# Token gates as one 256-column product per token, high and low part side by side, beside unpaired expert-up units

## The chip, the cores and the metric

The kernel runs on one core of a Trainium2 chip. The metric is device time in microseconds (us); lower is better. TensorE (PE) multiplies matrices: stationary weights are loaded (PEld) and the columns of the other operand stream through them into a PSUM bank (8 banks of 512 fp32 columns). VectorE (DVE), ScalarE (ACT) and GpSimd (POOL) do the elementwise work, SyncE (SP) issues the DMA loads. Each engine works its own list of instructions in order, and engines wait for each other on semaphores.

## The reference

Two transformer blocks over 256 tokens of width 1024. The first ones (attention, MLP, convolution, retention, block attention) are not touched. The last layer is a mixture of 16,384 single-neuron experts, addressed by a pair of keys (i1, i2) of 128 each; each token picks 16 experts per head of 8 heads:

```
def peer(h, w_q, sub_keys, u_tab, v_tab):
    ...
    experts = jnp.take_along_axis(cand_i, pos, axis=-1)      # i1 * 128 + i2, 128 per token
    gates = jax.nn.softmax(top_s, axis=-1).astype(h.dtype)
    def one_chunk(args):
        hc, ec, gc = args
        a = jax.nn.gelu(jnp.einsum('td,thkd->thk', hc, u_tab[ec]), approximate=False)
        return jnp.einsum('thk,thkd->td', gc * a, v_tab[ec])
```

## The kernel before, in words

All weights come as 540 "units" of 128x1024 fp32 through a ring of four slots. The kernel keeps fp32 accuracy with one-pass fp32r products: ACT rounds a unit to its high part (`unit_hi`, L488), POOL or DVE makes the low part as the difference (`unit_lo`, L494), and PE adds three products high x high, high x low, low x high. `h_tile` (L549) does so with 24 products of 256 columns.

Instead of gathering experts, the kernel computes all of them densely. `act_e` holds 128 tiles of 128 experts x 256 tokens: tile n holds gelu(h.u) of the experts whose second key is n. It is then multiplied by a dense matrix of gates, zero for experts not picked, and multiplied with the v table (128 units `peer_v`, L614).

The gate matrix of one token, 128 x 128, is the product of two one-hot matrices over its 128 picks: `hot1` (pick x first key) and `hot2` (pick x second key, times the gate). DVE builds them four tokens at a time, a *group* (`one_hots`, three operations of 512 elements; 64 groups, two buffers in turn), PE multiplies (`token_gates`, L1255, four products of 128 columns in plain fp32), and DVE applies the group to `act_e` (`gate_tokens`): it multiplies the tiles already there (units 0 to n-1) and copies the gates of the tiles still to come. Tiles that come later are multiplied as they arrive (`gate_unit`).

The order is written out by hand. Of the 128 expert-up units (`peer_u`), 44 run before any group. Then follow 84 *gated units* k = 0..83, with four groups in every five units (`groups_before`): PE does group, unit, group, unit, group, unit, group, unit, unit. A gated unit goes through `h_pair_tile`: 8 products of 512 columns (L561: the high part of the weights by the high and low part of h side by side) and 8 of 256 (L567). It leaves two halves in its bank, 4 or 5, which DVE adds (`unit_sum`, L2717) into bank 6 or 7, where ACT takes the gelu (L1793 for the tokens already gated, L1795 into `act_e` for the rest). The groups use PSUM banks 0, 1 and 2 in turn, one bank for each. On DVE an iteration is: wait for the group's bank, make the one-hots of group g+2 into the buffers that group g has left, `gate_tokens(g)`, `gate_unit(k-1)`, `unit_sum(k)`.

Of the kernel before, what the change touches and what calls it, by code (L numbers as in the profile page):

```python
# [25 lines left out]
ALU = mybir.AluOpType  # L26
# [3 lines left out]
P = 128  # L30
T = 256
# [17 lines left out]
HOT_BANKS = 3  # L49
# [163 lines left out]
def build(nc, stream, x_t, x_rows, ctx_t, params, consts, decay, lam_in, rel_bias, onehot, dist_mask, scale_w, aside_w, c_rows, ln_rows,  # L213
          bias_rows, gate_cols, out):
    with ExitStack() as ctx:
# [32 lines left out]
        h_span = rounded("h_span", "arena", [P, (at["h"] - at["arena"]) // 4 + KC * T])  # L248

        def h_part(like, skip=0):  # L250

            first = (at[like] - at["arena"]) // 4 + skip
            return h_span[:, first:first + KC * T].rearrange("p (a b) -> p a b", a=KC)

        h_lo = h_part("h")
        gate_r = rounded("gate_r", "gate_lo", [P, T])
        e_pair = rounded("e_pair", "late", [P, 4, 2 * T], 2048)
# [32 lines left out]
        h_hi_1, h_hi_2, h_hi_3 = h_part("arena", 10752), h_part("arena", 19456), h_part("late")  # L290
        def h_parts(like, skip):

            first = (at[like] - at["arena"]) // 4 + skip
            apart = (at["h"] - at["arena"]) // 4 - first
            views = []
            for kc in range(KC):
                a = h_span[:, first + kc * T:first + (kc + 1) * T]
                views.append(bass.AP(a.tensor, a.offset, [a.ap[0], [apart, 2], [1, T]]))
            return views

        h_parts_1, h_parts_2, h_parts_3 = h_parts("arena", 10752), h_parts("arena", 19456), h_parts("late", 0)
# [60 lines left out]
        hot1, hot2 = ([a[:, at:at + 4 * P].rearrange("p (t e) -> p t e", t=4) for a, at in places] for places in (  # L362
            ((late, 2048), (cst, CONST["cos_2d"])), ((late, 3072), (cst, CONST["mean_64"]))))
# [23 lines left out]
        gate_ps = ps[:, 3, P:P + T]  # L387
# [7 lines left out]
        iota16_ps = ps[:, 7, 0:TOPK]  # L395

# [77 lines left out]
        unit_gelu = sem("unit_gelu")  # L474
# [25 lines left out]
        def _(pe):  # L500
# [39 lines left out]
            def h_tile(u, h_hi, bank, i=None):  # L540

                w_hi, w_lo = split_unit(u, i)
                start_fill(bank)
                for w, x in ((w_hi, h_hi), (w_hi, h_lo), (w_lo, h_hi)):
                    if w is w_lo:
                        wait_unit_lo(u, i)
                    for kc in range(KC):
                        begin = w is w_hi and x is h_hi and kc == 0
                        m = pe.matmul(ps[:, bank, 0:T], w[:, kc * P:(kc + 1) * P], x[:, kc, :], start=begin,  # L549
                                      stop=w is w_lo and kc == KC - 1)  # L550
                        if begin:
                            m.then_inc(units_begun, 1)
                m.then_inc(full[bank], 1)
                fills[bank].add()

            def h_pair_tile(u, parts, h_hi, bank, i=None):

                w_hi, w_lo = split_unit(u, i)
                start_fill(bank)
                for kc in range(KC):  # L560
                    m = pe.matmul(ps[:, bank, :], w_hi[:, kc * P:(kc + 1) * P], parts[kc], start=kc == 0, stop=False,  # L561
                                  skip_group_check=True)
                    if kc == 0:
                        m.then_inc(units_begun, 1)
                wait_unit_lo(u, i)
                for kc in range(KC):
                    m = pe.matmul(ps[:, bank, 0:T], w_lo[:, kc * P:(kc + 1) * P], h_hi[:, kc, :], start=False,  # L567
                                  stop=kc == KC - 1, skip_group_check=True)
                m.then_inc(full[bank], 1)
                fills[bank].add()  # L570
# [655 lines left out]
            def peer_u_pair(n):  # L1226
                h_pair_tile(FIRST_UNIT["peer_u"] + n, h_parts_3, h_hi_3, 4 + n % 2)

# [20 lines left out]
            def token_gates(g):  # L1249

                b = g % HOT_BANKS
                pe.wait_ge(hot_ready, g + 1)
                start_fill(b)
                for t in range(4):
                    m = pe.matmul(ps[:, b, t * P:(t + 1) * P], hot1[g % 2][:, t, :], hot2[g % 2][:, t, :], start=True, stop=True)  # L1255
                m.then_inc(full[b], 1)
                fills[b].add()

            for k in range(GATED_UNITS):
                for g in groups_before(k):  # L1260
                    token_gates(g)
                peer_u_pair(FIRST_GATED + k)
# [36 lines left out]
        def _(act):  # L1299
# [486 lines left out]
            for k in range(GATED_UNITS):  # L1786
                n = FIRST_GATED + k
                b = 4 + n % 2
                t = tokens_gated(k)
                unit_hi(act, FIRST_UNIT["peer_u"] + n + 2)  # L1790
                act.wait_ge(emptied[b], drains[b].add())
                total = ps[:, 6 + k % 2, 0:T]
                m = act.activation(total[:, 0:t], total[:, 0:t], ACT.Gelu)  # L1793
                if t < T:
                    m = act.activation(act_e[:, n, t:T], total[:, t:T], ACT.Gelu)  # L1795
                m.then_inc(unit_gelu, 1)
                if k >= GATED_UNITS - 3:
                    expert_hi(k - (GATED_UNITS - 3))
# [14 lines left out]
        def _(dve):  # L1813
# [845 lines left out]
            step(dve.tensor_copy(gate_hi[:, :], ps[:, 6, 0:T]))  # L2659
            settle()  # L2660
            dve.tensor_copy(gate_ps, gate_hi[:, :]).then_inc(emptied[6], 1)
# [4 lines left out]

            def one_hots(g):

                def of_tokens(a):
                    return a[:, 4 * g:4 * g + 4].unsqueeze(2).broadcast_to([P, 4, P])  # L2670

                iotas = spread(iota_ps, 4)
                step(dve.tensor_tensor(hot2[g % 2], iotas, of_tokens(i2_t), ALU.is_equal))
                dve.tensor_tensor(hot1[g % 2], iotas, of_tokens(i1_t), ALU.is_equal)
                settle()
                dve.tensor_tensor(hot2[g % 2], hot2[g % 2], of_tokens(gate_ps), ALU.mult).then_inc(hot_ready, 1)

            def gate_tokens(g, units):

                b = g % HOT_BANKS  # L2680
                gates = ps[:, b, :].rearrange("p (t e) -> p e t", t=4)
                a = act_e[:, :, 4 * g:4 * g + 4]
                dve.tensor_tensor(a[:, 0:units], a[:, 0:units], gates[:, 0:units], ALU.mult)
                dve.tensor_copy(a[:, units:N_EXP], gates[:, units:N_EXP]).then_inc(emptied[b], 1)
# [4 lines left out]
            def gate_unit(k):  # L2689

                n = FIRST_GATED + k
                t = tokens_gated(k)
                dve.wait_ge(unit_gelu, k + 1)
                last_group = t // 4 - 1
                dve.wait_ge(emptied[last_group % HOT_BANKS], reads[last_group % HOT_BANKS].n)
                dve.tensor_tensor(act_e[:, n, 0:t], ps[:, 6 + k % 2, 0:t], act_e[:, n, 0:t],
                                  ALU.mult).then_inc(unit_gated, 1)

            for g in range(2):
                one_hots(g)  # L2700
# [11 lines left out]
            def unit_sum(k):  # L2712

                n = FIRST_GATED + k
                b = 4 + n % 2
                dve.wait_ge(full[b], n_u[n % 2].add())
                dve.tensor_reduce(ps[:, 6 + k % 2, 0:T], ps[:, b, :].rearrange("p (a t) -> p t a", a=2), AX_X,  # L2717
                                  ALU.add).then_inc(emptied[b], 1)

            for k in range(GATED_UNITS):  # L2720
                for g in groups_before(k):
                    filled(g % HOT_BANKS)
                    if g + 2 < GROUPS:
                        one_hots(g + 2)
                    if k >= 1:
                        dve.wait_ge(unit_gelu, k)
                    gate_tokens(g, FIRST_GATED + k)
                if k >= 1:
                    gate_unit(k - 1)
# [3 lines left out]
            gate_unit(GATED_UNITS - 1)  # L2733
# [294 lines left out]
```

## Time and profile before

| | |
|---|---|
| median of 3 runs | 1877.89 us (1874.55 to 1877.93) |
| the profiled execution | 1875.69 us, of which its span is 1873.9 us |
| PE busy in the span | 1814.3 us, 97% |
| DVE, ACT, POOL busy | 1204.1, 859.8, 997.0 us |
| the stage of groups and gated units | about 1227.9 to 1520.6 us of the span |
| mean granted TensorE clock | 0.991 of full speed |

Busy time says which engine is full, not which wait decides. A row of the timeline is one instruction or a run of equal ones: its start, how long it took from the first start to the last end, and in brackets how long the engine had been idle and who ended that. PE and DVE begin an instruction before the one in front of it has ended, so what an instruction adds to the time of its engine is the distance between two starts, which is less than its duration.

### The profile page before, as it was taken

The numbers are of one execution on the slowest core, as the hardware profiler recorded it, in microseconds if no ns is written. First come the engines' busy times: TensorE is split into PE (matmuls) and PEld (weight loads), VectorE is DVE, ScalarE is ACT, GpSimd is POOL, SyncE is SP. The second block draws the span as 40 slices with busy tenths as digits, with TensorE's granted clock in tenths as the row PEclk, the third lists the DMA queues.
The fourth block names the chain that finished last, engine by engine and source line by source line (L and its number), as shares of the span: only waits on it lengthen the run. The fifth ranks groups of instructions, "written<-read, shape, count | busy, mean of one in ns | idle before, by whom it ended". The sixth has DMA issues, their size and how long they took to land.

```text
span 1873.9 us, 30601 instructions
## 1 busy us (share of the span) xinstructions
PE 1814.3 (97%) x10910; PEld 1554.6 (83%) x10910; DVE 1204.1 (64%) x2053; ACT 859.8 (46%) x1407; POOL 997.0 (53%) x431
## 2 busy tenths in 40 slices
PE   5999899998999999999999999999999999999999
PEld 2847579887979997988978899998999988888887
DVE  6587767788556545133233269978888867777776
ACT  3033554445445554542453546643344345554453
POOL 4043146443775444675438668876666654444443
PEclk8999999999999999999999999999999999999999
DMA  8787247786655554543324455544444455555554
GB/s 322 260 299 253 72 146 243 263 277 218 210 202 178 186 186 157 191 147 101 113 90 169 157 171 183 185 146 147 155 150 146 153 184 191 192 195 195 190 191 168
DMA packets 95319, 345.98 MB, mean 185 GB/s; under 512 B 10544, under 2 KB 12032, under 8 KB 94592
## 3 DMA queue, kind: packets, MB, share of 16 engines
q1 hardware_dynamic: 78048, 283.67, 45.2%
q10 hardware_dynamic: 17184, 61.11, 9.5%
q8 instruction: 59, 0.97, 0.2%
q14 instruction: 28, 0.23, 0.0%
HBM read 343.66 MB, written 1.08 MB: 184 GB/s over the span
## 4 chain that ended last, share of the span: by engine, by line
PE 82%; DVE 5%; issue 4%; DMA 4%; POOL 2%; ACT 2%; ACTq 0%; DVEq 0%; POOLq 0%; SPq 0%
PE ps L614 27%; PE ps L549 24%; PE ps L561 8%; PE ps L567 4%; PE ps L1255 3%; POOL ring_lo L494 2%; PE ps L770 2%; PE ps L837 2%; DMA ring<-stream 2%; PE ps L684 1%; PE ps L1000 1%; PE ps L533 1%; DMA arena<-aside_w 1%; DMA cst<-consts 1%; PE ps L784 1%
## 5 line engine op out<-in xcount | busy, mean ns | idle before, releaser
L494 POOL TENSOR_TENSOR ring_lo<-ring,ring_hi 128x1024 fp32r<-128x1024 f32 x371 | 896.8, 2422 | 691.7 <-ACT ring_hi L488 690.4
L488 ACT ACTIVATE ring_hi<-ring 128x1024 fp32r<-128x1024 f32 x502 | 531.2, 1059 | 442.5 <-DMA ring<-stream 438.5
L549 PE MATMUL ps<-h_span,ring_hi 128*128 128x256 f32 x2848 | 377.3, 286 | 0.2
L549 PEld LDWEIGHTS ps<-h_span,ring_hi 128*128 128x128 f32 x2848 | 360.5, 193 | 9.2 <-issue 4.7
L614 PE MATMUL ps<-ring_hi,e_pair 128*128 128x512 f32 x1024 | 253.8, 389 | 0.9 <-DVE e_pair L2707 0.9
L2707 DVE TENSOR_TENSOR e_pair<-arena,e_pair 128x256 fp32r<-128x256 f32 x128 | 174.9, 1367 | 99.3 <-ACT e_pair L1784 99.2
L614 PEld LDWEIGHTS ps<-ring_hi,e_pair 128*128 128x128 f32 x1024 | 192.1, 188 | 41.1 <-issue 1.3
L549 PE MATMUL ps<-h_span,ring_lo 128*128 128x256 f32 x1424 | 200.7, 284 | 0.7 <-POOL ring_lo L494 0.7
L494 DVE TENSOR_TENSOR ring_lo<-ring,ring_hi 128x1024 fp32r<-128x1024 f32 x141 | 175.5, 1245 | 37.5 <-ACT ring_hi L488 37.2
L549 PEld LDWEIGHTS ps<-h_span,ring_lo 128*128 128x128 f32 x1424 | 184.2, 193 | 1.5 <-POOL ring_lo L494 1.5
L614 PE MATMUL ps<-ring_hi,arena_r 128*128 128x512 f32 x672 | 174.5, 392 | 0.7 <-ACT ring_hi L488 0.7
L561 PE MATMUL ps<-h_span,ring_hi 128*128 128x512 f32 x672 | 174.6, 402 | 0.0
L2324 DVE CAST arena_r<-arena 128x256 fp32r<-128x256 f32 x64 | 78.1, 1220 | 111.8 <-ACT arena L1625 111.6
L614 PEld LDWEIGHTS ps<-ring_hi,arena_r 128*128 128x128 f32 x672 | 122.3, 189 | 24.5 <-ACT ring_hi L488 1.1
L561 PEld LDWEIGHTS ps<-h_span,ring_hi 128*128 128x128 f32 x672 | 120.3, 189 | 22.1
L614 PE MATMUL ps<-ring_lo,e_pair 128*128 128x512 f32 x512 | 137.5, 389 | 0.0
L614 PEld LDWEIGHTS ps<-ring_lo,e_pair 128*128 128x128 f32 x512 | 96.2, 188 | 19.9
L1793 ACT ACTIVATE ps<-ps 128x256 f32<-128x256 f32 (+39 forms) x84 | 22.6, 269 | 175.2 <-DVE ps L2717 175.2
L1337 ACT ACTIVATE arena<-ps 128x256 f32<-128x256 f32 (+2 forms) x118 | 45.4, 385 | 122.8 <-PE ps L549 111.0
L567 PEld LDWEIGHTS ps<-h_span,ring_lo 128*128 128x128 f32 x672 | 91.6, 189 | 7.2
L614 PE MATMUL ps<-ring_lo,arena_r 128*128 128x512 f32 x320 | 91.2, 393 | 4.8 <-POOL ring_lo L494 2.4
L567 PE MATMUL ps<-h_span,ring_lo 128*128 128x256 f32 x672 | 93.4, 282 | 0.0
(289 smaller groups left out, 2217.8 us busy)
## 6 DMA issues: line engine op xcount, KB each, us to landing
ring<-stream SPq DMA_DIRECT2D x540, 512.0 KB, 3.3
arena<-aside_w ACTq DMA_DIRECT2D x49, 512.0 KB, 4.7
late<-aside_w ACTq DMA_DIRECT2D x21, 512.0 KB, 5.1
resid<-aside_w ACTq DMA_DIRECT2D x10, 512.0 KB, 6.2
arena<-scale_w ACTq DMA_DIRECT2D x8, 512.0 KB, 16.0
arena<-ln_rows ACTq DMA_DIRECT2D x8, 512.0 KB, 5.0
arena<-gate_cols ACTq DMA_DIRECT2D x2, 1024.0 KB, 4.8
arena<-decay ACTq DMA_DIRECT2D x1, 1536.0 KB, 7.0
```

Source lines behind the costliest of these rows:

```text
L488: act.activation(ring_hi[:, s, :], ring[:, s, :], ACT.Copy).then_inc(hi_ready, 1)
L494: eng.tensor_tensor(ring_lo[:, s, :], ring[:, s, :], ring_hi[:, s, :], ALU.subtract).then_inc(lo_ready[s], 1)
L549: m = pe.matmul(ps[:, bank, 0:T], w[:, kc * P:(kc + 1) * P], x[:, kc, :], start=begin, stop=w is w_lo and kc == KC - 1)
L561: m = pe.matmul(ps[:, bank, :], w_hi[:, kc * P:(kc + 1) * P], parts[kc], start=kc == 0, stop=False, skip_group_check=True)
L567: m = pe.matmul(ps[:, bank, 0:T], w_lo[:, kc * P:(kc + 1) * P], h_hi[:, kc, :], start=False, stop=kc == KC - 1, skip_group_check=True)
L614: m = pe.matmul(ps[:, b, :], x[:, tt * P:(tt + 1) * P], w[:, half * 512:(half + 1) * 512], start=start, stop=stop, skip_group_check=True)
L770: m = pe.matmul(ps[:, bank, tt * P:(tt + 1) * P], hcat[:, kc, tt * P:(tt + 1) * P], w[:, kc * P:(kc + 1) * P], start=kc == 0, stop=kc == K ...
L837: m = pe.matmul(ps[:, b0 + tt, :], x[:, kc, tt * P:(tt + 1) * P], w[:, k2 * 512:(k2 + 1) * 512], start=begin and kc == 0, stop=w is w_lo a ...
L1255: m = pe.matmul(ps[:, b, t * P:(t + 1) * P], hot1[g % 2][:, t, :], hot2[g % 2][:, t, :], start=True, stop=True)
L1337: act.activation(dst, ps[:, b, 0:n], func, **kw).then_inc(emptied[b], 1)
L2324: dve.tensor_copy(hid_hi[:, j % 4, :], hid2[:, j % 4, :]).then_inc(hid_hi_ready, 1)
L2707: dve.tensor_tensor(e_lo[:, e % 4, :], act_e[:, e if row is None else row, :], e_hi[:, e % 4, :], ALU.subtract).then_inc(e_lo_ready, 1)
```

## The change

- `token_gates`: `hot2` now has 256 columns per token, the one-hot times the high part of the gate and the one-hot times its low part, all fp32r. The product of a token has 256 columns, so a group of four tokens fills two banks. The three banks are taken in pairs (0,1), (2,0), (1,2): each group shares its second bank with the group before it.
- `one_hots` has four operations of 512 elements where it had three; the gates lie in PSUM for half of the tokens at a time (`half_gates`, called twice).
- ACT copies the high halves out of PSUM: for tiles already there into a buffer `gate_part`, for the others into `act_e`.
- `gate_tokens` adds the low halves to the copies (two operations) and then multiplies. In groups whose banks are not neighbours (one in three) each operation is done in two pieces. The lower bank is freed by the multiplication, the higher one by a further step after it.
- The gated units go through `h_tile` (24 products of 256 columns) like all others. `unit_sum` is gone: ACT takes the gelu straight from bank 4 or 5. `gate_unit(k)` now stands in the same iteration as unit k.

```diff
-HOT_BANKS = 3
+HOT_BANKS = ((0, 1), (2, 0), (1, 2))
...
             def token_gates(g):
-                b = g % HOT_BANKS
                 pe.wait_ge(hot_ready, g + 1)
-                start_fill(b)
-                for t in range(4):
-                    m = pe.matmul(ps[:, b, t * P:(t + 1) * P], hot1[g % 2][:, t, :], hot2[g % 2][:, t, :], start=True, stop=True)
-                m.then_inc(full[b], 1)
-                fills[b].add()
+                for b in HOT_BANKS[g % 3]:
+                    start_fill(b)
+                    first = 2 * (b == max(HOT_BANKS[g % 3]))
+                    for t in range(2):
+                        m = pe.matmul(ps[:, b, t * T:(t + 1) * T], hot1[g % 2][:, first + t, :],
+                                      hot2_parts[g % 2][:, first + t, :], start=True, stop=True)
+                    m.then_inc(full[b], 1)
+                    fills[b].add()
...
-                peer_u_pair(FIRST_GATED + k)
+                peer_u_tile(FIRST_GATED + k)
...   (ACT)
+                for g in groups_before(k):
+                    for hb in HOT_BANKS[g % 3]:
+                        act.wait_ge(full[hb], mark["group", g][hb])
...
+                    for hi, _, tokens, part in group_parts(g):
+                        act.activation(part[:, 0:n], hi[:, 0:n], ACT.Copy)
+                        m = act.activation(tokens[:, n:N_EXP], hi[:, n:N_EXP], ACT.Copy)
+                    m.then_inc(group_copied, 1)
                 unit_hi(act, FIRST_UNIT["peer_u"] + n + 2)
-                act.wait_ge(emptied[b], drains[b].add())
-                total = ps[:, 6 + k % 2, 0:T]
-                m = act.activation(total[:, 0:t], total[:, 0:t], ACT.Gelu)
+                act.wait_ge(full[b], drains[b].add())
+                if k >= 2:
+                    act.wait_ge(unit_gated, k - 1)
+                m = act.activation(ps[:, 6 + k % 2, 0:t], ps[:, b, 0:t], ACT.Gelu)
...   (DVE)
-                dve.tensor_tensor(hot2[g % 2], hot2[g % 2], of_tokens(gate_ps), ALU.mult).then_inc(hot_ready, 1)
+                dve.tensor_tensor(lo, hi, of_tokens(gate_lo_ps, 4 * g % P), ALU.mult)
+                dve.tensor_tensor(hi, hi, of_tokens(gate_hi_ps, 4 * g % P), ALU.mult).then_inc(hot_ready, 1)
 
             def gate_tokens(g, units):
-                dve.tensor_tensor(a[:, 0:units], a[:, 0:units], gates[:, 0:units], ALU.mult)
-                dve.tensor_copy(a[:, units:N_EXP], gates[:, units:N_EXP]).then_inc(emptied[b], 1)
+                dve.wait_ge(group_copied, g + 1)
+                for hi, lo, a, part in group_parts(g):
+                    step(dve.tensor_tensor(hi[:, 0:units], lo[:, 0:units], part[:, 0:units], ALU.add))
+                for hi, lo, a, part in group_parts(g):
+                    dve.tensor_tensor(a[:, units:N_EXP], lo[:, units:N_EXP], a[:, units:N_EXP], ALU.add)
+                settle()
+                for hi, lo, a, part in group_parts(g):
+                    m = dve.tensor_tensor(a[:, 0:units], hi[:, 0:units], a[:, 0:units], ALU.mult)
+                m.then_inc(emptied[low], 1)
+                dve.wait_ge(emptied[low], mark["group", g][low])
+                dve.sem_inc(emptied[high], 1)
...
             for k in range(GATED_UNITS):
                 for g in groups_before(k):
-                    filled(g % HOT_BANKS)
+                    for b in HOT_BANKS[g % 3]:
+                        dve.wait_ge(full[b], mark["group", g][b])
                     if g + 2 < GROUPS:
                         one_hots(g + 2)
...
-                unit_sum(k)
+                gate_unit(k)
```

On PE, a group and the unit behind it, before (`late` holds the one-hots of a group; `emptied1` is bank 1 free again; `h_span` holds both parts of h):

```order
L1255 MATMUL ps<-late 128x128 [waits emptied2,hot_ready]
L1255 MATMUL ps<-late 128x128 x3
L561 MATMUL ps<-h_span,ring_hi 128x512 [waits emptied4,hi_ready]
L561 MATMUL ps<-h_span,ring_hi 128x512 x7
```

and of the changed kernel (`hot_parts` is the two-part `hot2`, `hot` is `hot1`, `late_r` and `h_lo` the two parts of h), a group, its unit and the group behind that:

```order
L1235 MATMUL ps<-hot_parts_a,hot_a 128x256 [waits emptied2,hot_ready]
L1235 MATMUL ps<-hot_parts_a,hot_a 128x256
L1235 MATMUL ps<-hot_parts_a,hot_a 128x256 [waits emptied0]
L1235 MATMUL ps<-hot_parts_a,hot_a 128x256
L547 MATMUL ps<-late_r,ring_hi 128x256 [waits emptied5,hi_ready]
L547 MATMUL ps<-late_r,ring_hi 128x256 x7
L547 MATMUL ps<-h_lo,ring_hi 128x256 x8
L547 MATMUL ps<-late_r,ring_lo 128x256 [waits lo_ready1]
L547 MATMUL ps<-late_r,ring_lo 128x256 x7
L1235 MATMUL ps<-hot_parts_b,hot_b 128x256 [waits emptied1,hot_ready]
L1235 MATMUL ps<-hot_parts_b,hot_b 128x256
L1235 MATMUL ps<-hot_parts_b,hot_b 128x256 [waits emptied2]
```

The four products of a group had one wait on a bank; now the third has a wait of its own, on the bank that the group before it used.

On DVE, one iteration before (tile 54, a group in it):

```order
L2673 TENSOR_TENSOR late<-ps,late 128x512 [waits full2]
L2674 TENSOR_TENSOR late<-ps,late 128x512
L2676 TENSOR_TENSOR late<-late,ps 128x512 [waits dve_step]
L2683 TENSOR_TENSOR arena<-arena,ps 128x54x4 [waits unit_gelu]
L2684 COPY arena<-ps 128x74x4
L2696 TENSOR_TENSOR arena<-ps,arena 128x32 [waits emptied1,unit_gelu]
L2717 TENSOR_REDUCE ps<-ps 128x256 [waits full4]
```

and of the changed kernel (a group with neighbouring banks):

```order
L2674 TENSOR_TENSOR hot_parts_b<-ps,late 128x4x128 [waits full1,full0]
L2675 TENSOR_TENSOR hot_b<-ps,late 128x512
L2677 TENSOR_TENSOR hot_parts_b<-hot_parts_b,ps 128x4x128 [waits dve_step]
L2678 TENSOR_TENSOR hot_parts_b<-hot_parts_b,ps 128x4x128
L2685 TENSOR_TENSOR ps<-ps,gate_part 128x77x4 [waits group_copied]
L2687 TENSOR_TENSOR arena<-ps,arena 128x51x4
L2690 TENSOR_TENSOR arena<-ps,arena 128x77x4 [waits dve_step]
L2706 TENSOR_TENSOR arena<-ps,arena 128x112 [waits emptied0,emptied5]
```

The operation that frees a bank of the group was the fifth (the copy) and is the seventh now; all that stand in front of it wait until the whole group is out of PE.

## Rows read from the trace of the kernel before

**Rows 1.** The page: span, busy time of the engines.
```profile
span 1873.9 us, 30601 instructions
PE 1814.3 (97%) x10910; PEld 1554.6 (83%) x10910; DVE 1204.1 (64%) x2053; ACT 859.8 (46%) x1407; POOL 997.0 (53%) x431
```

**Rows 2.** Busy time by stretch (us): engines, granted clock, DMA.
```profile
1240.00:1280.00 40.00, 40.00 (x252) 35.81 (x251) 32.07 (x68) 16.42 (x36) 26.34 (x12) 1.00 0.45 148
1440.00:1480.00 40.00, 40.00 (x255) 35.93 (x255) 34.72 (x69) 16.44 (x36) 27.31 (x12) 1.00 0.45 145
920.00:960.00 40.00, 37.29 (x243) 29.79 (x241) 12.34 (x38) 19.89 (x50) 15.25 (x7) 1.00 0.27 93
```

**Rows 3.** PE's timeline in the stage: start, length, instruction.
```profile
1227.92 1.06 PE L1255 MATMUL ps<-late 128*128 128x128 f32 x8
...
1301.99 1.05 PE L1255 MATMUL ps<-cst 128*128 128x128 f32 x8
1302.79 2.11 PE L561 MATMUL ps<-h_span,ring_hi 128*128 128x512 f32 x8
1304.74 1.11 PE L567 MATMUL ps<-h_span,ring_lo 128*128 128x256 f32 x8
1305.69 1.06 PE L1255 MATMUL ps<-late 128*128 128x128 f32 x8
...
1506.62 2.00 PE L561 MATMUL ps<-h_span,ring_hi 128*128 128x512 f32 x8
1508.46 1.12 PE L567 MATMUL ps<-h_span,ring_lo 128*128 128x256 f32 x8
1509.41 2.00 PE L561 MATMUL ps<-h_span,ring_hi 128*128 128x512 f32 x8
...
1520.59 2.00 PE L614 MATMUL ps<-ring_hi,e_pair 128*128 128x512 f32 x8
```

**Rows 4.** PE's timeline among the ungated, unpaired units.
```profile
1150.41 1.12 PE L549 MATMUL ps<-h_span,ring_lo 128*128 128x256 f32 x8
1151.37 2.08 PE L549 MATMUL ps<-h_span,ring_hi 128*128 128x256 f32 x16
1153.29 0.40 PE L549 MATMUL ps<-h_span,ring_lo 128*128 128x256 f32 x2
```

**Rows 5.** DVE's timeline, one iteration of the middle of the stage.
```profile
1303.08 0.69 DVE L2673 TENSOR_TENSOR cst<-ps,late 128x512 f32<-128x512 f32 x1 [0.19 <-PE ps L1255]
1303.68 0.68 DVE L2674 TENSOR_TENSOR cst<-ps,late 128x512 f32<-128x512 f32 x1
1304.28 0.68 DVE L2676 TENSOR_TENSOR cst<-cst,ps 128x512 f32<-128x512 f32 x1
1304.88 0.42 DVE L2683 TENSOR_TENSOR arena<-arena,ps 128x260 f32<-128x260 f32 x1
1305.21 0.41 DVE L2684 COPY arena<-ps 128x252 f32<-128x252 f32 x1
1305.54 0.22 DVE L2696 TENSOR_TENSOR arena<-ps,arena 128x68 f32<-128x68 f32 x1
1305.89 0.70 DVE L2717 TENSOR_REDUCE ps<-ps 128x256 f32<-128x512 f32 x1
```

**Rows 6.** DVE's timeline late in the stage.
```profile
1494.71 0.64 DVE L2683 TENSOR_TENSOR arena<-arena,ps 128x476 f32<-128x476 f32 x1
1495.27 0.19 DVE L2684 COPY arena<-ps 128x36 f32<-128x36 f32 x1
1495.38 0.40 DVE L2696 TENSOR_TENSOR arena<-ps,arena 128x240 f32<-128x240 f32 x1
```

**Rows 7.** ACT's timeline in the middle of the stage.
```profile
1302.92 0.21 ACT L1793 ACTIVATE ps<-ps 128x68 f32<-128x68 f32 x1 [2.30 <-DVE ps L2717]
1303.04 0.32 ACT L1795 ACTIVATE arena<-ps 128x188 f32<-128x188 f32 x1
1303.25 1.06 ACT L488 ACTIVATE ring_hi<-ring 128x1024 fp32r<-128x1024 f32 x1
```

**Rows 8.** The timeline around PE's restart after a wait on DVE.
```profile
1218.51 2.30 DVE L2652 TENSOR_TENSOR cst<-cst,small 128x128 f32<-128x128 f32 x1
1220.87 0.66 PE L1242 MATMUL ps<-cst 128*128 128x128 f32 x4 [0.22 <-DVE cst L2652]
```

**Rows 9.** DVE's timeline ahead of the first group.
```profile
1226.48 0.68 DVE L2676 TENSOR_TENSOR cst<-cst,ps 128x512 f32<-128x512 f32 x1
1229.11 0.69 DVE L2673 TENSOR_TENSOR late<-ps,late 128x512 f32<-128x512 f32 x1 [1.95 <-PE ps L1255]
```

More of the change, by code:

```diff
@@ L247, in build @@
         late_r = rounded("late_r", "late", [P, 2048])
[L248 to L255, printed above, removed]
+        h_lo = rounded("h_lo", "h", [P, KC, T])
         gate_r = rounded("gate_r", "gate_lo", [P, T])
+        hot2_parts = [rounded("hot2_parts_a", "late", [P, 4, 2 * P], 2048), rounded("hot2_parts_b", "cst", [P, 4, 2 * P], CONST["cos_2d"])]
+        hot1 = [rounded("hot1_a", "late", [P, 4, P], 3072), rounded("hot1_b", "cst", [P, 4, P], CONST["mean_64"])]
+        gate_part = sb("gate_part", [P, N_EXP, 4])
         e_pair = rounded("e_pair", "late", [P, 4, 2 * T], 2048)
@@ L288, in build @@
         rstd = area(30720, 2, 512)
[L290 to L301, printed above, removed]
+        h_hi_1 = arena_r[:, 10752:12800].rearrange("p (a b) -> p a b", a=KC)
+        h_hi_2 = arena_r[:, 19456:21504].rearrange("p (a b) -> p a b", a=KC)
+        h_hi_3 = late_r[:, :].rearrange("p (a b) -> p a b", a=KC)
         hid_hi = arena_r[:, 12800:13824].rearrange("p (a b) -> p a b", a=4)
@@ L386, in build @@
         iota_ps = ps[:, 3, 0:P]
-        gate_ps = ps[:, 3, P:P + T]
+        gate_hi_ps, gate_lo_ps = ps[:, 3, P:2 * P], ps[:, 3, 2 * P:3 * P]
         bn = ps[:, 4, 384:408].rearrange("p (t a b) -> p t a b", t=2, a=2)
@@ L395, in build, with group_parts @@
         iota16_ps = ps[:, 7, 0:TOPK]
+        def group_parts(g):
+            low, high = min(HOT_BANKS[g % 3]), max(HOT_BANKS[g % 3])
+            banks = [(low, 2)] if high == low + 1 else [(low, 1), (high, 1)]
+            views, first = [], 0
+            for bank, n in banks:
+                parts = ps[:, bank:bank + n, :].rearrange("p b (t a e) -> p e (b t) a", t=2, a=2)
+                tokens = slice(4 * g + first, 4 * g + first + 2 * n)
+                views.append((parts[:, :, :, 0], parts[:, :, :, 1], act_e[:, :, tokens], gate_part[:, :, first:first + 2 * n]))
+                first += 2 * n
+            return views
         landed = [sem(f"landed{s}") for s in range(RING)]
@@ L473, in build @@
         unit_gated = sem("unit_gated")
-        unit_gelu = sem("unit_gelu")
+        group_copied = sem("group_copied")
         dve_rows = sem("dve_rows")
@@ L552, in h_tile @@
                             m.then_inc(units_begun, 1)
[L553 to L568, printed above, removed]
                 m.then_inc(full[bank], 1)
@@ L1249, in token_gates @@
             def token_gates(g):
-                b = g % HOT_BANKS
                 pe.wait_ge(hot_ready, g + 1)
-                start_fill(b)
-                for t in range(4):
-                    m = pe.matmul(ps[:, b, t * P:(t + 1) * P], hot1[g % 2][:, t, :], hot2[g % 2][:, t, :], start=True, stop=True)
-                m.then_inc(full[b], 1)
-                fills[b].add()
+                for b in HOT_BANKS[g % 3]:
[6 more added lines that the diff above has]
+                    fills[b].add()
+                mark["group", g] = [fills[b].n for b in range(3)]
             for k in range(GATED_UNITS):
@@ L2665, in _, with half_gates, of_tokens @@
             dve.wait_ge(emptied[6], reads[6].n)
+            def half_gates(tt):
+                c = slice(tt * P, (tt + 1) * P)
+                dve.tensor_copy(gate_hi_ps, gate_hi[:, c])
+                step(dve.tensor_copy(gate_lo_ps, gate_lo[:, c]))
             def one_hots(g):
-                def of_tokens(a):
-                    return a[:, 4 * g:4 * g + 4].unsqueeze(2).broadcast_to([P, 4, P])
+                def of_tokens(a, first=4 * g):
+                    return a[:, first:first + 4].unsqueeze(2).broadcast_to([P, 4, P])
@@ L2678, in gate_tokens @@
+                dve.tensor_tensor(hi, hi, of_tokens(gate_hi_ps, 4 * g % P), ALU.mult).then_inc(hot_ready, 1)
             def gate_tokens(g, units):
[L2680 to L2684 removed]
+                low, high = min(HOT_BANKS[g % 3]), max(HOT_BANKS[g % 3])
@@ L2692, in gate_unit @@
                 t = tokens_gated(k)
-                dve.wait_ge(unit_gelu, k + 1)
+                dve.wait_ge(emptied[4 + n % 2], n_u[n % 2].add())
                 last_group = t // 4 - 1
-                dve.wait_ge(emptied[last_group % HOT_BANKS], reads[last_group % HOT_BANKS].n)
+                b = min(HOT_BANKS[last_group % 3])
+                dve.wait_ge(emptied[b], mark["group", last_group][b])
                 dve.tensor_tensor(act_e[:, n, 0:t], ps[:, 6 + k % 2, 0:t], act_e[:, n, 0:t],
                                   ALU.mult).then_inc(unit_gated, 1)
+            half_gates(0)
+            settle()
             for g in range(2):
@@ L2710, in expert_lo @@
                     unit_lo(dve, FIRST_UNIT["peer_v"] + e, i)
[L2712 to L2718, printed above, removed]
             for k in range(GATED_UNITS):
                 for g in groups_before(k):
-                    filled(g % HOT_BANKS)
+                    for b in HOT_BANKS[g % 3]:
+                        dve.wait_ge(full[b], mark["group", g][b])
+                    if g + 2 == GROUPS // 2:
+                        half_gates(1)
+                        settle()
                     if g + 2 < GROUPS:
                         one_hots(g + 2)
-                    if k >= 1:
-                        dve.wait_ge(unit_gelu, k)
                     gate_tokens(g, FIRST_GATED + k)
-                if k >= 1:
-                    gate_unit(k - 1)
-                unit_sum(k)
+                gate_unit(k)
                 if k >= GATED_UNITS - 3:
                     expert_lo(k - (GATED_UNITS - 3))
-            gate_unit(GATED_UNITS - 1)
             for e in range(3, 8):
```

21 lines of the change are left out of this document (11 added, 10 removed).

## The prediction

> **What bounds the kernel now.** I read the page first: PE is busy for 97% of the span, DVE for 64% [rows 1]. Then the stretches of the stage that is changed: in 40 us PE is busy for 40.00, at the full granted clock; DVE has 32 to 35 of 40, ACT 16, POOL 26 to 27 [rows 2]. So nothing but PE's own work sets the time of this stage, and DVE is the engine with the least room. PE's timeline gives the prices. From a group to the next it takes 1305.69 - 1301.99 = 3.70 us, one unit in between; without a group a unit takes 1509.41 - 1506.62 = 2.79 [rows 3]. So a group costs 0.91 us of PE. As a check, 84 units at 2.79 and 64 groups at 0.91 are 292.6; the stage lasts from 1227.92 to 1520.59, 292.7 [rows 3]. An unpaired unit of 24 products of 256 columns takes 1153.29 - 1150.41 = 2.88, 0.12 per product [rows 4].
>
> **PE's own work.** The trace has no fp32r product of one-hots; the nearest row is the 256-column product at 0.12 [rows 4]. A group of four is then 0.48 in place of 0.91: 64 x 0.43 = 27.5 us less. The bounds: it can't be much under 0.12 (the 512-column products have 0.23), and at worst it stays at 0.91, which I price below. Unpairing costs 84 x (2.88 - 2.79) = 7.6 us. The net for PE alone is -19.9 us. If nothing made PE wait, the time would be 1875.7 - 19.9 = 1855.8.
>
> **The work of DVE per group.** What an operation costs is the distance between starts: 0.60 for 512 elements, 0.33 for 260 or 252, 0.56 and 0.11 for 476 and 36 [rows 5, 6]. That is about 0.065 us and 1.04 ns per element; the end comes 0.09 after the next could start. All new forms (an add of PSUM and an SBUF buffer into PSUM or `act_e`) have one operand in PSUM and one in SBUF, as L2676 and L2683 have, and I take them at this rate. Gone is `unit_sum`, 0.6 per unit. New per group: a fourth one-hot operation (+0.60), and two adds and a multiplication where a multiplication and a copy were. With n tiles there (44 to 127, mean 84): adds of 4n and 512 - 4n elements, 0.41 + 0.25, then the multiplication of 4n, 0.41 to its next start and 0.50 to its end.
>
> **The new wait.** This decides, and it is not a matter of DVE's sum but of one loop. The second half of a group needs the bank that it shares with the group before, and DVE frees that bank only when it has applied the whole group. DVE starts on a group when both banks are full, a moment that I call F; and it makes the one-hots of group g+2 first. So the bank is freed at F + 4 x 0.60 (one-hots) + 0.41 + 0.25 (adds) + 0.50 (multiplication) = F + 3.56 at mean n; at n = 44 it is F + 3.34, at n = 124 F + 3.78. When does PE want it? F is 0.04 after the end of the last group product (DVE starts at 1303.08 on a group whose record runs from 1301.99 for 1.05 [rows 3, 5]). That product began 0.32 before F (a 256-column product takes 0.28 from start to end: 1.12 for eight at 0.12 [rows 4]), so the unit starts at F - 0.20, ends its pitch at F + 2.68, and two products later, at F + 2.92, PE comes to the third product of the next group. After a stalled group it is F + 2.86, since a product after a wait runs some 0.06 longer: the transposes at 1220.87 took 0.66 for four [rows 8]. PE restarts 0.05 after DVE's end (1218.51 + 2.30 = 1220.81 to 1220.87 [rows 8]). The wait is 3.56 + 0.05 - 2.86 = 0.75. One group in three works in halves (three more operations, 3 x 0.06) and hands on its higher bank, which is freed one step later (about 0.10, an estimate, bounds 0 and 0.2): +0.28 for a third of the groups, +0.09 in the mean. So 0.84 us for each wait.
>
> How often? Of the 64 groups, 48 come one unit behind the last group. For the other 16 there are two units in between, PE arrives 2.88 later, and there is no wait. 48 x 0.84 = 40.3 us. Behind the waiting product on PE stands the unit, and behind it everything; before, PE had no idle time here, so the wait goes into the end in full.
>
> **Small terms.** Behind a unit without a group DVE has to wait for ACT's gelu before `gate_unit`, which now stands in front of the next group: gelu is some 0.48 after the unit's end, as in rows 7 (0.44 from L1793's start to L1795's end), and `gate_unit` takes 0.06 to 0.33 (rows 6: 0.40 long for 240 elements). DVE is then late at a group by 0.02 to 0.26: 16 x 0.14 = 2.2. `half_gates(1)` adds 0.4 once. Ahead of the first group DVE gets four operations of one-hots twice instead of three and three more small ones, about 2.6 us in all; it was through at 1226.48 + 0.68 and waited for the group till 1229.11 [rows 9], so it comes some 0.7 us, at most 1.2 us, late to group 0: +1.2. Sum 3.8.
>
> **What hides.** ACT's copies of a group take 0.07 + 0.75 ns per element, by the start distances of L1793 and L1795 (0.12 for 68, 0.21 for 188 [rows 7]): 0.5 to 0.7 us, from F on. DVE asks for them at F + 2.40, so 1.7 us are to spare, and ACT's whole iteration (copies 0.6, `unit_hi` 1.06, gelu 0.44) is 2.1 of some 4. `unit_hi` comes 0.6 later, for a unit that is two units ahead; POOL's low part behind it too. Nothing changes in SP's queue but that the loads follow the slower units. In the stage behind (L614) nothing moves.
>
> **Sum.** -19.9 + 40.3 + 3.8 = +24.2 us, on the profiled execution's 1875.7: 1899.9. That execution lies 2.2 us under the median of the runs, 1877.9, so I keep to it within that and predict 1900.
>
> The Trainium skill ("VectorE: DVE Perf Modes", The DRAIN you can't avoid) says that the next VectorE operation can't issue before the pipe of the last one is empty. Here rows 5 say otherwise: L2674 starts at 1303.68 while L2673 runs till 1303.77. By the rule each of the seven operations would cost its full duration, 0.09 more, so some 0.5 us more per wait and 24 us in all; by the rows it costs nothing. The trace decides for the known forms, but where an operation waits on the one before it a part of this could come back, which is the first rival.
>
> **Rivals.**
> - *The hand-overs on DVE cost more.* The add that is waited for by the multiplication, the wait for ACT and the wait on its own result each cost a full end-to-start, 0.09 more than I count: 3 x 0.09 x 48 = 13 us, 1913. For: DVE has three waits inside `gate_tokens` where it had one. Against: the wait inside the one-hots costs nothing in rows 5 (0.60 again). Chance 0.15.
> - *The bank is free in time (faster).* If DVE were done by F + 2.8, PE would never wait and the gain of the products would stay: 1856. It decides from 0.75 us less than my chain has, that is more than one whole 512-element operation. For: DVE's sum per five units, 4 x (2.40 + 0.66 + 0.41) + 5 x 0.2 = 14.9, is under PE's 5 x 2.88 + 4 x 0.48 = 16.3, so an account by busy time says that it fits. Against: DVE can't begin before both banks are full, and rows 5 leave no room in the prices. Chance 0.10.
> - *Half of it.* If DVE's fixed part is 0.4 us less per group than I think, the waits lose 19 us and the result is 1881, about no change: 0.06.
> - *The one-hot products stay as long as they were.* PE's own work then falls by nothing on this term (+27.5), but PE arrives at the third product 0.2 later and fills the second half 0.2 later: the loop gets 0.21 longer, the 16 free groups 0.43: 1875.7 + 7.6 + 48 x (0.84 - 0.43 + 0.21) + 3.8 = 1917. Against: fp32r products of 256 columns have 0.12 in all of rows 4. Chance 0.04.
>
> The forecast itself has 0.65. What a measurement of this kernel can tell from no change is about 0.2%, 3.8 us. Faster by more than that: 0.11; within: 0.05; slower: 0.84. The forecast's own range is 1890 to 1910 (start distance 0.04 instead of 0.065 per operation gives -10; each hand-over between engines at nothing -7; +0.1 on each wait gives +5, +0.2 +10). With the cases at its sides I give 1882 to 1915.
>
> **What would show it.** Right: idle time of PE in front of the third of four group products, put down to DVE's multiplication in `gate_tokens`, some 0.6 us early and 1.1 us late in the stage, 48 times, 0 for groups after two units; group products 0.12 apart; the stage about 317 us long where it had 292.7. The granted clock stays full: PE's idle pieces are under 1.5 us, and with 7% idle it was 1.00 before [rows 2]. Wrong: PE without gaps there and a stage of 273 us; gaps in front of units (L547, which would be ACT's or POOL's doing) rather than of group products; or a DVE that waits for `group_copied`.

## The result

The changed kernel takes 1902.4 us (median of 4 runs, 1898.6 to 1904.3) against 1876.2 before (1870.8 to 1877.9): a ratio of 1.0139, with a 95% interval of 1.0116 to 1.0162. It is 1.4% slower. The forecast was 1900, with 1882 to 1915 as its range.

The page of the changed kernel, against [rows 1]: PE is busy for 8 us less, and the span is 25 us longer. So what was added is not work of PE but idle time.

```profile
span 1899.3 us, 31987 instructions
...
PE 1806.5 (95%) x11326; PEld 1564.5 (82%) x11326; DVE 1229.5 (65%) x2165; ACT 907.0 (48%) x1577; POOL 996.9 (52%) x431
```

The same stretches as in [rows 2], busy time of PE, PEld, DVE, ACT and POOL, then granted clock, DMA share and GB/s:

```profile
1240.00:1280.00 40.00, 36.55 (x295) 35.34 (x294) 31.77 (x79) 21.42 (x55) 24.68 (x12) 1.00 0.40 139
...
1440.00:1480.00 40.00, 34.97 (x281) 33.75 (x280) 33.73 (x75) 19.81 (x52) 24.63 (x11) 1.00 0.42 141
```

PE was busy for 40.00 of 40 before; it is now for 36.6 early and 35.0 late in the stage, at the full clock. DVE has no more busy time than before in these stretches, since it waits too. Who PE waits for, from 1225 to 1560 us (sum, times, longest):

```profile
PE ps L1235 <- DVE arena L2690: 21.5, 31, 1.2
PE ps L1235 <- DVEq L2693: 14.6, 16, 1.2
```

These are all of PE's waits in the stage: 47, all in front of a group product (L1235), 31 for the multiplication in `gate_tokens` (L2690), which frees the lower bank of a pair, and 16 for the step behind it (L2693), which frees the higher one. PE's timeline over two groups with two units before the first of them, to be put beside [rows 3]:

```profile
1379.22 0.64 PE L1235 MATMUL ps<-hot_parts_a,hot_a 128*128 128x256 f32 x4
1379.70 1.12 PE L547 MATMUL ps<-late_r,ring_hi 128*128 128x256 f32 x8
1380.66 1.12 PE L547 MATMUL ps<-h_lo,ring_hi 128*128 128x256 f32 x8
1381.62 1.12 PE L547 MATMUL ps<-late_r,ring_lo 128*128 128x256 f32 x8
1382.58 0.39 PE L1235 MATMUL ps<-hot_parts_b,hot_b 128*128 128x256 f32 x2
1383.72 0.51 PE L1235 MATMUL ps<-hot_parts_b,hot_b 128*128 128x256 f32 x2 [0.74 <-DVE arena L2690]
```

DVE's rows of the same stretch, which answer to [rows 5]:

```profile
1380.11 0.68 DVE L2674 TENSOR_TENSOR hot_parts_a<-ps,late 128x512 fp32r<-128x512 f32 x1
1380.71 0.68 DVE L2675 TENSOR_TENSOR hot_a<-ps,late 128x512 fp32r<-128x512 f32 x1
1381.31 0.68 DVE L2677 TENSOR_TENSOR hot_parts_a<-hot_parts_a,ps 128x512 fp32r<-128x512 f32 x1
1381.90 0.68 DVE L2678 TENSOR_TENSOR hot_parts_a<-hot_parts_a,ps 128x512 fp32r<-128x512 f32 x1
1382.50 0.51 DVE L2685 TENSOR_TENSOR ps<-ps,gate_part 128x336 f32<-128x336 f32 x1
1382.92 0.33 DVE L2687 TENSOR_TENSOR arena<-ps,arena 128x176 f32<-128x176 f32 x1
1383.17 0.50 DVE L2690 TENSOR_TENSOR arena<-ps,arena 128x336 f32<-128x336 f32 x1
```

The first group comes through in one piece, four products in 1379.70 - 1379.22 = 0.48 us: the products are as cheap as hoped. DVE starts on it at 1380.11 (0.2 us late, behind a `gate_unit`) and needs 3.56 us to the end of the multiplication at 1383.67. PE has been through the unit and two products of the next group by 1382.82 and starts the third at 1383.72, 0.90 us later; the bracket says 0.74, since it counts from the end of the product in front, not from where the next could have started.

### The profile page after: what moved, and what is told of

Read it like the earlier page. It is cut to its first block, busy times and chain, and to the rows that moved or that the text cites. A ratio compares the mean times of both kernels' runs of the same rounds, so it can differ in the third digit from the quotient of the medians.

```text
span 1899.3 us, 31987 instructions
## 1 busy us (share of the span) xinstructions
PE 1806.5 (95%) x11326; PEld 1564.5 (82%) x11326; DVE 1229.5 (65%) x2165; ACT 907.0 (48%) x1577; POOL 996.9 (52%) x431
## 4 chain that ended last, share of the span: by engine, by line
PE 78%; DVE 13%; DMA 3%; issue 2%; ACT 2%; POOL 2%; DVEq 0%; ACTq 0%; SPq 0%; POOLq 0%
PE ps L547 31%; PE ps L596 28%; PE ps L752 2%; PE ps L531 2%; PE ps L666 2%; PE ps L819 2%; POOL ring_lo L492 2%; PE ps L1235 2%; PE ps L766 2%; DMA ring<-stream 1%; PE ps L982 1%; DVE hot_parts_a L2674 1%; DVE ps L2685 1%; DVE arena L2690 1%; DVE hot_parts_a L2678 1%
## 5 line engine op out<-in xcount | busy, mean ns | idle before, releaser
L547 PE MATMUL ps<-h_lo,ring_hi 128*128 128x256 f32 x2096 | 295.2, 284 | 0.0
L547 PEld LDWEIGHTS ps<-h_lo,ring_hi 128*128 128x128 f32 x2096 | 271.4, 193 | 0.0
L547 PE MATMUL ps<-late_r,ring_lo 128*128 128x256 f32 x1136 | 159.4, 283 | 0.0
L547 PE MATMUL ps<-late_r,ring_hi 128*128 128x256 f32 x1136 | 159.4, 283 | 0.0
L547 PEld LDWEIGHTS ps<-late_r,ring_lo 128*128 128x128 f32 x1136 | 146.5, 192 | 0.2 <-POOL ring_lo L492 0.2
L547 PEld LDWEIGHTS ps<-late_r,ring_hi 128*128 128x128 f32 x1136 | 146.1, 191 | 0.2 <-issue 0.2
L547 PE MATMUL ps<-arena_r,ring_hi 128*128 128x256 f32 x960 | 139.5, 289 | 0.0
L547 PE MATMUL ps<-arena_r,ring_lo 128*128 128x256 f32 x960 | 135.2, 284 | 0.5 <-POOL ring_lo L492 0.5
L547 PEld LDWEIGHTS ps<-arena_r,ring_hi 128*128 128x128 f32 x960 | 128.8, 193 | 7.8 <-issue 3.4
L547 PEld LDWEIGHTS ps<-arena_r,ring_lo 128*128 128x128 f32 x960 | 124.1, 192 | 1.0 <-POOL ring_lo L492 1.0
L596 PEld LDWEIGHTS ps<-ring_lo,e_pair 128*128 128x128 f32 x512 | 96.1, 188 | 19.9
```

The source lines that it names most:

```text
L596: m = pe.matmul(ps[:, b, :], x[:, tt * P:(tt + 1) * P], w[:, half * 512:(half + 1) * 512], start=start, stop=stop, skip_group_check=True)
```

## The experiments

Theory A: the wait on the shared bank, 47 times, at the end of a chain that begins when the group is out of PE. Theory B: VectorE simply has too much work for the time PE needs. Stage means the time, in the profiled execution, from the first group product to the first product of the expert-down stage; "lost" is the sum of what the distances between PE's starts in it have over 0.12 us (left out where other forms of product stand in the stage). The two times of the kernel before are its medians beside e1 to e4 and beside e5 to e8, and the ratios go by the one that was measured together with the run.

| kernel | time, us | against before, 95% interval | stage, us | lost, us |
|---|---|---|---|---|
| before | 1875.8, 1876.9 | 1 | 292.7 | |
| changed | 1902.4 | 1.0139 (1.0116 to 1.0162) | 320.3 | 48.3 |
| e1 four banks | 1863.9 | 0.9937 (0.9920 to 0.9953) | 280.6 | 8.7 |
| e2 bank freed earlier | 1874.5 | 0.9990 (0.9975 to 1.0006) | 290.4 | 18.5 |
| e3 before, unpaired | 1882.6 | 1.0039 (1.0024 to 1.0053) | 298.8 | |
| e4 one more operation | 1930.4 | 1.0309 (1.0276 to 1.0342) | 352.0 | 79.6 |
| e5 four banks, paired | 1923.0 | 1.0243 (1.0226 to 1.0260) | 340.6 | |
| e6 applied first | 1867.5 | 0.9956 (0.9941 to 0.9971) | 282.6 | 10.6 |
| e7 no wait on own result | 1858.4 | 0.9904 (0.9888 to 0.9921) | 271.8 | 0 |
| e8 fewer groups late | 1856.0 | 0.9891 (0.9875 to 0.9908) | 271.8 | 0 |

### e1: no bank shared

```diff
-HOT_BANKS = ((0, 1), (2, 0), (1, 2))
+HOT_BANKS = ((0, 1), (2, 3))        # and g % 2 for g % 3
...
-        iota_ps = ps[:, 3, 0:P]
+        iota_ps = ps[:, 7, 0:P]       # the gates beside it, too
...
-                if k >= 2:
-                    act.wait_ge(unit_gated, k - 1)
-                m = act.activation(ps[:, 6 + k % 2, 0:t], ps[:, b, 0:t], ACT.Gelu)
+                if k >= 1:
+                    act.wait_ge(unit_gated, k)
+                m = act.activation(ps[:, 6, 0:t], ps[:, b, 0:t], ACT.Gelu)
```

> The changed kernel with four banks for the groups, in pairs (0,1) and (2,3), so that no group shares a bank with the group before it; the one-hot index row and the gates move to bank 7, and the gelus of the gated units all go through bank 6. VectorE's work is the same but for the operations in two pieces, which are gone (no pair is of distant banks). Theory A (PE waits because the third group product needs a bank that VectorE frees only at the end of its chain): the 47 waits go, PE's own work of 84 x 2.88 + 64 x 0.48 = 272.6 us is left of the stage's 320, so about 1855 us. Theory B (VectorE has more work than fits beside PE, whichever bank is used): the time stays within 6 us of the changed kernel, 1896 or more. Theory C (half and half: the bank is free, but VectorE's sum late in the stage, some 16.9 us for 16.3 of PE per five units, holds PE there): 1860 to 1870, with all waits after the middle of the stage.

Measured: 1863.9 us, 38 us under the changed kernel. The 47 waits are gone; what is left of PE's waits from the first group on is one line (10 waits, in front of the first product of a group), and the stretches of 100 us say where:

```profile
PE ps L1235 <- DVE arena L2690: 5.4, 10, 0.7
```

```profile
1300.00:1400.00 100.00, 99.46 (x829) 99.09 (x828) 90.72 (x199) 55.13 (x139) 72.02 (x30) 1.00 0.49 162
1400.00:1500.00 100.00, 94.89 (x774) 92.98 (x774) 88.58 (x182) 52.39 (x130) 68.96 (x29) 1.00 0.45 149
```

So A is right for 40 of the 48 us lost, and C, the mixed case, for the rest: 7.7 of the 8.7 us lost lie behind 1400 us, where a group costs VectorE most. B alone is out: the work was the same but for the pieces, which were some 0.2 us in every third group.

### e2: the bank freed earlier, the work unchanged

```diff
                     if g + 2 < GROUPS:
-                        one_hots(g + 2)
+                        one_hots(g + 2, range(2))
                     gate_tokens(g, FIRST_GATED + k)
+                    if g + 2 < GROUPS:
+                        one_hots(g + 2, range(2, 4))
```

(`ops` says which of the four one-hot operations are issued. A wait of VectorE for its earlier one-hots, once, ahead of `half_gates(1)`, belongs to the edit, too.)

> The changed kernel with the four one-hot operations cut in two: two of them before the group is applied, two after it. The three banks and the work stay as they are; only the bank is freed 2 x 0.60 us earlier. Theory A: the mean wait of 0.93 us (44 us in 47 waits) all but goes; left are the groups whose banks are not neighbours, late in the stage, 5 to 15 us in all, so 1860 to 1873 us. Theory B: 1900, as VectorE's sum is unchanged.

Measured: 1874.5, 28 us under the changed kernel, by nothing but order, and not clear of the kernel before (the interval takes in 1). It is 1.5 us over the range of A: 32 waits of 0.47 on the average are left, the more the further into the stage. A group in two pieces late in the stage shows it, and the row on PE behind it:

```profile
1444.12 0.65 DVE L2694 TENSOR_TENSOR arena<-ps,arena 128x210 f32<-128x210 f32 x2
```

```profile
1444.88 0.50 PE L1235 MATMUL ps<-hot_parts_a,hot_a 128*128 128x256 f32 x2 [0.67 <-DVEq L2697]
```

The pieces end at 1444.77, the higher bank is passed on 0.1 later, and PE, whose second product started at 1443.93, could have gone on at 1444.05. What the expectation left out is that the two operations put behind the release stand ahead of the next group: VectorE starts on this group at 1442.13, 1.0 us after its last product's end (1441.11), where it needed 0.1 in the changed kernel. So late in the stage most of the 1.2 us comes back as a later start, and VectorE's sum begins to decide.

### e3: the unpairing alone

```diff
-                peer_u_pair(FIRST_GATED + k)
+                peer_u_tile(FIRST_GATED + k)
...   (ACT)
+                act.wait_ge(full[b], drains[b].add())
+                m = act.activation(ps[:, 6 + k % 2, 0:t], ps[:, b, 0:t], ACT.Gelu)
...   (DVE)
-                unit_sum(k)
```

> The kernel before with the expert-up units unpaired alone: 24 products of 256 columns per gated unit, ScalarE takes the gelu straight from the unit's bank, VectorE's sum of the halves is gone; the groups stay as they are (one bank, plain fp32). By theory A and B alike it costs PE 84 x 0.09 = 7.6 us: 1884 us (1881 to 1887), no PE wait in the stage. If the unpaired units cost nothing beside fp32 groups: 1876.

Measured: 1882.6, 6.7 us more than before; its stage is 6.1 us longer. PE stays full, and VectorE has 24 us of 40 where it had 32:

```profile
1240.00:1280.00 40.00, 40.00 (x341) 40.00 (x340) 24.16 (x56) 16.86 (x35) 26.53 (x12) 1.00 0.44 146
```

This is the price that buys room on VectorE: 6 to 7 us of PE for 84 x 0.60 = 50 us of VectorE.

### e4: one more operation in the chain

```diff
                 step(dve.tensor_tensor(hi, iotas, of_tokens(i2_t), ALU.is_equal))
+                step(dve.tensor_tensor(lo, iotas, of_tokens(i2_t), ALU.is_equal))
```

> The changed kernel with a fifth one-hot operation of 512 elements per group (a comparison that the next operation overwrites), 0.60 us more on VectorE before the bank is freed. Theory A: each of the 46 to 48 waits gets 0.60 us longer, and the groups behind two units do not: +28 us, 1930. Theory B (VectorE's sum decides): each of the 62 groups gets 0.60 longer: +37 us, 1939. If VectorE did not decide at all: 1902.

Measured: 1930.4 us, +28.0 against the changed kernel, as A said (B said +37). PE's waits in the stage:

```profile
PE ps L1235 <- DVE arena L2691: 39.2, 29, 3.0
PE ps L1235 <- DVEq L2694: 22.9, 15, 1.8
```

Compared group by group, a wait is 0.60 us longer than in the changed kernel (the median of 44), and the groups behind two units wait for nothing in either, where B would have them wait, too. That tells A from B better than the time does. In sum the waits in front of the third product went from 43.4 us (47) to 69.1 (44). The other three, of groups 2, 27 and 54, have no wait since PE came late to them, slowed by a stretch at half its clock (see the last section). These stretches cost 5.7 us, and so this execution's stage is 31.7 us longer and not 26; its time is only 27.8 longer, as the stage began 4.0 us earlier.

### e5: the unpairing undone, on four banks

```diff
-                peer_u_tile(FIRST_GATED + k)
+                h_pair_tile(FIRST_UNIT["peer_u"] + FIRST_GATED + k, h_parts_3, h_hi_3, 4 + (FIRST_GATED + k) % 2)
...   (DVE)
+                    if k >= 1:
+                        dve.wait_ge(unit_gelu, k)
                     gate_tokens(g, FIRST_GATED + k)
-                gate_unit(k)
+                if k >= 1:
+                    gate_unit(k - 1)
+                unit_sum(k)
```

> The four-bank kernel (e1) with the unpairing undone: gated units again as 8 products of 512 and 8 of 256 columns, VectorE adds their halves (0.60 us per unit), ScalarE takes the gelu from the sum. PE's own work falls by 84 x 0.09 = 7 us. If PE alone decided: 1857. Theory A with C (VectorE's sum holds PE in the last third already): VectorE has 4 x 4.0 + 5 x 0.85 = 20.3 us per five units, against PE's 15.9, so PE waits throughout and the stage takes some 16 x 20.3 + 12 = 337 us: 1920 (1900 to 1940).

Measured: 1923.0, 59 us over e1, where PE had 7 us less to do. VectorE is the bound now. Its busy time does not tell: it is 90.5 of 100 us, as in e1 (90.7). But it no longer waits for PE; in these 100 us its waits are 4.3 us for its own results and 2.6 for ScalarE's gelu. PE waits for the sum of the halves (L2762), which frees a unit's bank:

```profile
1300.00:1400.00 100.00, 82.20 (x474) 70.76 (x473) 90.54 (x190) 44.03 (x112) 59.48 (x25) 1.00 0.41 132
```

```profile
PE ps L576 <- DVE ps L2762: 17.4, 15, 2.3
PE ps L1268 <- DVE arena L2721: 0.2, 1, 0.2
```

So wide gates and paired units don't go together in this order of VectorE's work, even with four banks; the unpairing is no side issue.

### e6: the group applied before any one-hot

The edit of e2 with `range(0)` ahead of `gate_tokens` and all four operations behind it.

> The changed kernel (three banks) with no one-hot operation before the group is applied and all four after it. The bank is freed 2.4 us earlier than in the changed kernel, but VectorE now waits for ScalarE's copies (some 0.75 us after the group) at each group. Theory A: no wait on the shared bank: 1862 to 1868, what is left being VectorE's sum. Theory B (VectorE's sum alone decides, and it is longer here by the waits for ScalarE): over 1900.

Measured: 1867.5. With three banks and the same operations, order alone takes 35 us off the changed kernel. The time is in A's range, but A had no wait on the shared bank, and 18 are left, 8.4 us, all from group 19 on: late in the stage VectorE now comes to most groups 2.0 to 2.3 us after their end, as it is still at the one-hots put behind the release (behind two units it is 0.9 to 1.0, the wait for ScalarE's copies). That each order of the same operations gives another time, 1902, 1874 or 1867, rules out B as the only cause.

### e7 and e8: the rest of VectorE's idle time

In e1 `gate_unit` stands 0.21 us behind the multiplication in front of it, since VectorE waits there for its own result:

```profile
1486.65 0.65 DVE L2690 TENSOR_TENSOR arena<-ps,arena 128x476 f32<-128x476 f32 x1
1487.52 0.41 DVE L2706 TENSOR_TENSOR arena<-ps,arena 128x244 f32<-128x244 f32 x1 [0.21 <-DVE arena L2690]
```

```diff
-                dve.wait_ge(emptied[low], mark["group", g][low])
-                dve.sem_inc(emptied[high], 1)      # PE takes the lower bank's release for both
+                if g >= GROUPS - 2:
+                    dve.wait_ge(emptied[low], mark["group", g][low])
+                    dve.sem_inc(emptied[high], GROUPS // 2)
...
-                dve.wait_ge(emptied[b], mark["group", last_group][b])
+                dve.wait_ge(rest_added, last_group + 1)
```

> The four-bank kernel (e1) without VectorE's wait for its own multiplication (0.21 us idle in front of gate_unit, 64 times): the lower bank's release stands for both banks, and gate_unit waits on the add instead. e1 loses 8.7 us of PE in 27 gaps, 7.7 of them in the last 100 us, where VectorE is the full engine. If so, 0.2 us per group there gives back most: 1857 to 1860. If the gaps are of another origin: 1864.

Measured: 1858.4, and not one wait of PE from the first group to the end of the stage, late in it neither:

```profile
1400.00:1500.00 100.00, 100.00 (x838) 100.00 (x837) 87.25 (x182) 58.54 (x135) 72.67 (x31) 1.00 0.50 165
```

Its 84 units and 64 groups take 271.8 us, which is PE's own work. e8 spreads the groups by another rule:

```diff
+def groups_up_to(k):
+    return min(GROUPS, -(-(900 * k - 13 * k * k // 10) // 1000))
...
-    return range(-(-4 * k // 5), min(GROUPS, -(-4 * (k + 1) // 5)))
+    return range(groups_up_to(k), groups_up_to(k + 1))
...
```

> e7 with the 64 groups spread another way over the first 81 gated units: nine in ten units at the beginning, seven in ten at the end, instead of four in five throughout, since a group costs VectorE 3.3 us at the beginning and 3.65 at the end. If VectorE's sum late in the stage is all that is left, no gap remains and PE's own work stands alone: 1855 to 1857. If the early groups, now with fewer units between them, overfill VectorE there: 1860 or more.

Measured: 1856.0, the same as e7 within their runs (e7 1855.98 to 1858.58, e8 1855.37 to 1864.99), with the same stage of 271.8 us. As e7 had no gap left, there was nothing for the other spreading to win, and this run says nothing on whether it would help where gaps are left. Both beat the kernel before by 1.0 to 1.1%.

## Why the prediction was right

The forecast was 1900 by one mechanism, and that mechanism is what the trace shows and the runs bear out. The time came closer than the terms did, by some luck: the stage is 320.3 - 292.7 = 27.7 us longer, where 24.2 were forecast (PE's own work fell by 1.0 more, the waits cost 4.2 more), but the profiled execution as a whole is only 1901.1 - 1875.7 = 25.4 longer. Term by term:

- *The group products, -27.5 us.* Right: from e3 to e7 the stage falls from 298.8 to 271.8, 27.0 us, and the two differ on PE in the group products alone.
- *The unpairing, +7.6 us.* Right, if a little too high: 6.1 us of stage, 6.7 of time in e3. PE's own work together was forecast at -19.9 and is 271.8 - 292.7 = -20.9.
- *VectorE's prices.* Right: F + 3.56 to the end of the multiplication at n = 84 is 1383.67 - 1380.11 = 3.56. For the two ends of the stage the forecast's own rate gives 3.40 and 3.73, not its 3.34 and 3.78; measured are 3.41 (group 3) and 3.72 (group 59). An operation that waits for another costs no more than the rest (the multiplication L2690, which waits for L2685, starts 0.25 behind L2687, the price of 176 elements). The first rival, dearer hand-overs on DVE, had its place in one spot only: 0.21 us idle in front of `gate_unit`, 62 times. It lies behind the release of the bank and cost PE nothing in nearly all groups, as DVE was back before the next group was out: it started 0.11 us after the end of 44 of the 46 stalled groups that have one-hots behind them. The other two are group 30 (`half_gates(1)`) and group 58 (0.33).
- *The waits, 48 x 0.84 us and 3.8 us besides, 44.1.* Mis-sized by a tenth: 48.3 us. There were 47 of them, as group 62 has no one-hots to make any more and the last group finds its bank free, at 0.92 us in front of the third product and 0.10 at the fourth, whose start is 0.22 behind the third's and not 0.12. I had taken 0.06 for a restart from four transposes [rows 8]; it is 0.10, and DVE comes to a stalled group 0.11 after PE's end, not 0.04.
- *How often.* Right: no wait for the groups behind two units (1379.22 above), growing from 0.6 us at the beginning of the stage (0.9 where the higher bank is waited for) to between 0.9 and 1.4 at its end, a third of them for the step on the higher bank (16 of 47). The first wait, 1.36 us, was the longest early one, as the late start of DVE had it.
- *The other rivals.* The bank is not free in time, and the busy-time account behind that rival (14.9 of 16.3 us per five units) shows its limit: that sum was about right (VectorE is busy for 90.7 of 100 us in the middle of e1's stage, where PE hardly waits, which is 14.8 of 16.3), and still the kernel lost 48 us, since work that can't start before F does not fill the time before F. The half-way case did not come, nor did products as long as before: a group takes 0.48 us.
- *The paragraph on the Trainium skill.* It left something out: the section that it names ("VectorE: DVE Perf Modes", The DRAIN you can't avoid) goes on to say that a next operation which is not held starts earlier. So the 24 us don't follow from the Trainium skill, and rows 5 don't contradict it. Here, too, operations overlap: L2685 starts at 1382.50, while L2678 runs till 1382.58.

So the change was a good trade lost to one bank: it saves PE 21 us of work and costs it 48 of waiting.

## What to carry to other kernels

An engine with room by its busy time can still hold the bound engine, if the release that this one waits for stands last in a chain that only starts when its previous piece is done; reckon the chain from the moment its input is full to the release, and compare it with the time until the buffer is wanted again. When an output gets twice as wide, look first at which buffers are now shared between neighbours, then at whether work that does not depend on the new input stands ahead of the release: here a fourth bank (with which the operations in pieces go, too) was worth 38 us and a better order alone 28 or 35 us. What is moved behind the release comes ahead of the next piece, though, so order alone helps as long as the engine has room. And an engine's wait for its own last result is cheap only while it has room (0.21 us, 64 times: 5.5 us in e7 against e1).

## What the runs showed of the hardware

In e4 and e5, where PE waits longest, the granted clock was not full throughout the stage. In e4's profiled execution it is 1.2 GHz in four short stretches, the first of them right behind the first wait, which was 3.0 us long:

```profile
1229.06 0.51 PE L1235 MATMUL ps<-hot_parts_b,hot_b 128*128 128x256 f32 x2 [3.00 <-DVE arena L2691]
1229.41 1.75 PE L547 MATMUL ps<-late_r,ring_hi 128*128 128x256 f32 x8
1230.96 1.91 PE L547 MATMUL ps<-h_lo,ring_hi 128*128 128x256 f32 x8
1232.66 1.26 PE L547 MATMUL ps<-late_r,ring_lo 128*128 128x256 f32 x8
...
1234.33 1.12 PE L547 MATMUL ps<-late_r,ring_hi 128*128 128x256 f32 x8
```

Eight products take 1.55 and 1.70 us from start to start there, and 0.96 at 2.4 GHz. In the four stretches some 60 products start 0.21 us apart in place of 0.12, 5.7 us in all. The whole stage of e4, and that of the changed kernel:

```profile
1222.00:1574.00 352.00, 289.85 (x2274) 280.86 (x2274) 293.48 (x659) 164.05 (x418) 198.62 (x84) 0.98 0.38 126
```

```profile
1226.00:1547.00 321.00, 284.96 (x2279) 275.42 (x2278) 255.04 (x595) 164.46 (x419) 199.19 (x84) 1.00 0.41 139
```

The mean granted clock of the stage is 0.98 in e4 and 1.00 in the changed kernel, whose longest idle piece of PE there is 1.2 us. e5 has four such stretches as well, from 1432 us on. All eight begin at most 1.5 us after PE went on from a wait of 1.7 to 3.0 us; but e5 has five more waits as long behind which the clock stayed full. What exactly sets them off was not tried.
